# First block: inputs laid out in runs per partition, a new order of loads and modulation units, dummy matmuls

## The reference, cut to what matters

```python
mod = jax.nn.silu(c) @ w_ada[l] + b_ada[l]                      # c: 1 x 1024, w_ada: 1024 x 6144
sh1, sc1, g1, sh2, sc2, g2 = jnp.split(mod, N_MOD, axis=-1)     # six rows of 1024
h = rms_norm(x, norm1_g[l]) * (1.0 + sc1[:, None]) + sh1[:, None]   # x: 512 x 1024
z = h @ w_in[l]                                                 # the first input projection, 1024 x 2048
...
a_out = diff_attention(q, k, v, lam, subln_g[l], lambda_init)   # rotates parts of q and k by cos and sin first
p_out = multiscale_pool(u, w_pool[l], pool_scale[l])
mix = jnp.concatenate([a_out, p_out], axis=-1) @ w_out[l]
```

## Time and profile before

| what | us |
|---|---|
| median of three executions | 1986.4 |
| lowest and highest of them | 1984.96, 1988.44 |
| the profiled execution, its own time | 1988.75 |
| its span, first to last instruction | 1986.9 |
| TensorE busy in it | 1720.8 (87%) |
| VectorE, ACT, GpSimd busy | 856.9, 647.4, 243.6 |

### The profile page before, as it was taken

How to read it: one execution, slowest core, us unless ns; L and a number is a source line. 1 busy time by engine, 2 the same in 40 slices (tenths; PEclk the granted TensorE clock), 3 DMA queues, 4 the chain that set the end, 5 groups by cost and what they waited for, 6 DMA issues and landing times.

```text
span 1986.9 us, 44239 instructions
## 1 busy us (share of the span) xinstructions
PE 1720.8 (87%) x17970; PEld 990.3 (50%) x17970; DVE 856.9 (43%) x1514; ACT 647.4 (33%) x1218; POOL 243.6 (12%) x270
## 2 busy tenths in 40 slices
PE   5998895978777777897889789999988898899996
PEld 2444543544444444444765674354446755753452
DVE  1567524111111111377765763151357747642331
ACT  3414521000000000235544535252245526523442
POOL 0002211111111111005112100001002103000001
PEclk9998996999999999899999999999999999999998
DMA  9758015999999999611000003110211000012101
GB/s 357 264 200 292 1 63 220 383 423 424 424 424 424 424 424 419 236 63 45 4 3 2 3 9 122 43 43 32 80 43 34 4 2 2 4 65 105 43 1 42
DMA packets 75099, 307.76 MB, mean 155 GB/s; under 512 B 10908, under 2 KB 22300, under 8 KB 57888
## 3 DMA queue, kind: packets, MB, share of 16 engines
q1 hardware_dynamic: 63280, 291.98, 37.4%
q0 software_dynamic: 5360, 9.33, 1.3%
q10 hardware_dynamic: 6272, 3.81, 0.7%
HBM read 301.01 MB, written 16.52 MB: 160 GB/s over the span
## 4 chain that ended last, share of the span: by engine, by line
PE 72%; DVE 13%; another core or an unknown queue 6%; ACT 4%; issue 3%; ACTq 1%; DMA 1%; DVEq 0%; POOL 0%; POOLq 0%
PE bank L496 12%; PE bank L2271 12%; PE bank L2287 6%; PE bank L1040 6%; PE bank L549 4%; PE bank L2109 3%; PE bank L2193 3%; PE bank L542 2%; PE bank L1011 2%; PE bank L512 2%; DVE arena L1614 2%; ACT arena L1052 1%; PE bank L2121 1%; PE bank L2133 1%
## 5 line engine op out<-in xcount | busy, mean ns | idle before, releaser
L496 PE MATMUL bank<-hT,arena 128*128 128x512 f32 (+1 forms) x640 | 286.3, 603 | 3.8 <-ACTq L1053 2.4
L2271 PE MATMUL bank<-arena 128*64 128x256 f32 x1792 | 216.8, 399 | 71.2 <-remote 71.2
L2271 PEld LDWEIGHTS bank<-arena 128*64 128x64 f32 x1792 | 134.9, 143 | 163.0 <-issue 113.1
L496 PEld LDWEIGHTS bank<-hT,arena 128*128 128x128 f32 (+1 forms) x640 | 122.4, 193 | 160.4 <-issue 155.9
L2877 DVE COPY arena<-bank 128x256 f32<-128x256 f32 x32 | 13.6, 425 | 329.7 <-PE bank L2279 329.7
L542 PE MATMUL bank<-arena 64*64 64x64 f32 x3200 | 115.1, 223 | 6.8 <-ACT arena L1112 6.0
L2287 PE MATMUL bank<-arena 128*64 128x512 f32 x448 | 102.3, 598 | 16.4 <-remote 16.4
L2531 ACT ACTIVATE arena<-bank 128x512 f32<-128x512 f32 x32 | 19.1, 597 | 293.0 <-PE bank L2287 293.0
L542 PEld LDWEIGHTS bank<-arena 64*64 64x64 f32 x3200 | 105.2, 137 | 13.3 <-issue 6.9
L1052 ACT ACTIVATE arena<-bank 128x512 f32<-128x512 f32 (+2 forms) x124 | 73.2, 590 | 118.5 <-PE bank L496 79.1
L1040 PE MATMUL bank<-arena 128*128 128x512 f32 x256 | 110.4, 593 | 0.0
(11 more groups left out here) (452 smaller groups left out, 2775.4 us busy)
## 6 DMA issues: line engine op xcount, KB each, us to landing
arena<-w_gate SPq DMA_DIRECT2D x28, 2048.0 KB, 30.5
arena<-w_up SPq DMA_DIRECT2D x28, 2048.0 KB, 21.1
arena<-w_down SPq DMA_DIRECT2D x28, 2048.0 KB, 26.3
arena<-w_ada SPq DMA_DIRECT2D x12, 2048.0 KB, 20.0
arena<-w_in SPq DMA_DIRECT2D x10, 2048.0 KB, 9.3
arena<-w_out SPq DMA_DIRECT2D x6, 2048.0 KB, 7.8
arena<-w_in SPq DMA_DIRECT2D x6, 1536.0 KB, 6.5
hT<-w_up SPq DMA_DIRECT2D x4, 2048.0 KB, 20.9
```

Of the source, the lines that this page charges most:

```text
L496: m = pe.matmul(bank[b][0:w, :], slot2(n)[:, k, c:c + w], hT[:, k, :], start=(k == 0), stop=(k == KD - 1))
L2271: mm = pe.matmul(bank[b][c * CAP:(c + 1) * CAP, 0:FE // 2], XT[j][:, k % 4, k // 4, :], e_slot(e_at(e, i), KD)[:, k, c * (FE // 2):(c + 1) ...
```

## The change

- The host lays out w_ada, w_in and w_out of the first block by units, so that a unit is one run of 16 KB in each partition. xT comes as two halves of four tiles, 8 KB in each partition. w_pool and the router's weights (now one tensor) are one run per partition too.
- SP issues the parameters, constants and r1 first, then the two halves of x, each with a semaphore of its own, then the units. ACT issues none of these any more.
- The first four units come in the order 2, 3, 0, 1. TensorE runs for each unit products and then columns, where it ran one unit's products ahead of the columns of the unit before.
- The scale units' columns go to bank 4, and VectorE copies their rows to `mod_rows`. The shift units keep ACT and bank 7. VectorE makes the gains and scales hT when the scale columns are there, and adds the bias of the shift columns afterwards (`shift_moved`).
- ACT squares the even tiles of xT, VectorE the odd ones.
- `keep_busy` adds matmuls of ones with c_sb into bank 7 whose result is not used: two ahead of the sum of squares, and two behind the columns of each scale unit.
- ACT's DMA issues for cos and sin, w_pool and the router's weights (now three) stand behind the eight shift adds.

The core of the diff (left out: renamed semaphores, the signature, and the router's wait, which counts one DMA instead of two):

```diff
--- before.py
+++ after.py
@@ -44,6 +44,8 @@
+SCALE_FIRST = (2, 3, 0, 1)
...
@@ -309,13 +311,13 @@
 
 
         def ada_unit(n):
-            return w_ada[0, :, n * 512:(n + 1) * 512].rearrange("(k p) n -> p k n", p=P)
+            return w_ada[n]
         def in_unit(n):
-            return w_in[0, :, n * 512:(n + 1) * 512].rearrange("(k p) n -> p k n", p=P)
+            return w_in[n]
         def out_unit(n):
-            return w_out[0, :, n * 512:(n + 1) * 512].rearrange("(k p) n -> p k n", p=P)
-        units = [ada_unit(n) for n in range(4)]
-        ada_at, in_at = list(range(4)), []
+            return w_out[n]
+        units = [ada_unit(n) for n in SCALE_FIRST]
+        ada_at, in_at = [SCALE_FIRST.index(n) for n in range(4)], []
         for n in range(4):
             in_at.append(len(units))
             ada_at += [len(units) + 1, len(units) + 2]
@@ -1903,10 +1905,14 @@
 
         @block.sync
         def _(sp):
-            sp.dma_start(xT[:], xT_d.rearrange("(k p) t -> p k t", p=P)).then_inc(sem("x_loaded"), 16)
+            sp.dma_start(p1[:], par1).then_inc(sem("params_loaded"), 16)
+            sp.dma_start(c_sb[:, 0:CN["cosA"][0]], cn[:, 0:CN["cosA"][0]]).then_inc(sem("params_loaded"), 16)
+            sp.dma_start(r1[:], row1.to_broadcast([P, N_R1])).then_inc(sem("params_loaded"), 16)
+            for half in range(2):
+                sp.dma_start(xT[:, 4 * half:4 * half + 4, :], xT_d[half]).then_inc(sem(f"x_loaded{half}"), 16)
             for n, u in enumerate(units):
                 take(sp, slot_free[n % SLOTS])
-                sp.dma_start(slot(n), u).then_inc(slot_full[n % SLOTS], 16)
+                sp.dma_start(ring[:, n % SLOTS, :], u).then_inc(slot_full[n % SLOTS], 16)
             sp.dma_start(y_d, zero_row.to_broadcast([2 * T, D])).then_inc(sem("y_loaded"), 16)
             def weights_unit(e, i, s):
                 w, c = ((w_gate, 1), (w_up, 1), (w_down, 2))[i]
@@ -2074,27 +2080,34 @@
                     q = 32 * (k % 4)
                     mm = pe.matmul(bank[b][q:q + 32, :], small[:, k:k + 1].to_broadcast([P, 32]), slot(ada_at[u])[:, k, :],
                                    start=(k < 4), stop=(k >= 4))
-                mm.then_inc(for_act[b], 1)
+                mm.then_inc((for_dve if u in SCALE_FIRST[:2] else for_act)[b], 1)
             def mod_columns(u):
 
                 take(pe, sem(f"wT_full{u % 2}"))
-                if u % 4 == 0:
-                    take(pe, bank_free[7])
+                b = 4 if u in SCALE_FIRST[:2] else 7
+                if u % 4 == 0 or u == SCALE_FIRST[0]:
+                    take(pe, bank_free[b])
                 for m in range(4):
                     col = 4 * (u % 4) + m
-                    mm = pe.matmul(bank[7][:, col:col + 1], mod_rows[:, u % 2, m * P:(m + 1) * P],
+                    mm = pe.matmul(bank[b][:, col:col + 1], mod_rows[:, u % 2, m * P:(m + 1) * P],
                                    quarters if u < 4 else ones[:, 0:1], start=True, stop=True)
-                if u % 4 == 3:
-                    mm.then_inc(for_dve[7], 1)
+                if u % 4 == 3 or u == SCALE_FIRST[3]:
+                    mm.then_inc(for_dve[b], 1)
                 elif u >= 4:
                     mm.then_inc(sem(f"wT_free{u % 2}"), 1)
 
+            def keep_busy(n):
+
+                pe.wait_ge(bank_free[7], 1)
+                for _ in range(n):
+                    pe.matmul(bank[7][:, :], ones, c_sb[:, 0:512], start=True, stop=True)
+            keep_busy(2)
             sumsq(1, KD, 0)
-            for u in range(4):
+            for u in SCALE_FIRST:
                 mod_products(u)
-                if u > 0:
-                    mod_columns(u - 1)
-            mod_columns(3)
+                mod_columns(u)
+                if u in SCALE_FIRST[:2]:
+                    keep_busy(2)
 
             for n in range(2):
                 s = in_at[n] % SLOTS
@@ -2344,10 +2357,7 @@
         @block.scalar
         def _(act):
             chain = Chain(act, sem("act_chain"))
-            act.dma_start(p1[:], par1).then_inc(sem("params_loaded"), 16)
             late_cols = CN["cosA"][0]
-            act.dma_start(c_sb[:, 0:late_cols], cn[:, 0:late_cols]).then_inc(sem("params_loaded"), 16)
-            act.dma_start(r1[:], row1.to_broadcast([P, N_R1])).then_inc(sem("params_loaded"), 16)
             act.wait_ge(sem("params_loaded"), 48)
             act.activation(small[:, 0:8], par("c", 0, 8), ACT.Silu).then_inc(sem("silu_c"), 1)
 
@@ -2377,19 +2387,21 @@
                 act.sem_inc(slot_free[ada_at[u] % SLOTS], 1)
                 act.sem_inc(sem(f"wT_full{u % 2}"), 1)
 
-            act.wait_ge(sem("x_loaded"), 16)
-            squares(lambda i: xT[:, i, :], KD)
+            for i in range(0, KD, 2):
+                if i % 4 == 0:
+                    act.wait_ge(sem(f"x_loaded{i // 4}"), 16)
+                take(act, sem("sq_free0"))
+                act.activation(sq[:, 0, :], xT[:, i, :], ACT.Square).then_inc(sem("sq_full0"), 1)
             inverse_root(1, 1.0 / D)
-            for u in range(4):
+            for u in SCALE_FIRST[2:]:
                 mod_moved(u)
-            act.dma_start(c_sb[:, late_cols:], cn[:, late_cols:]).then_inc(sem("pool_w_loaded"), 16)
-            act.dma_start(pool_w[:], w_pool[0].rearrange("g c d -> c g d")).then_inc(sem("pool_w_loaded"), 16)
-            act.dma_start(w_router[:, :, 0:4], w_rg[0].rearrange("(k p) n -> p k n", p=P)).then_inc(sem("router_loaded"), 16)
-            act.dma_start(w_router[:, :, 4:36], w_re[0].rearrange("(k p) n -> p k n", p=P)).then_inc(sem("router_loaded"), 16)
-            act.wait_ge(sem("mod_ready"), 1)
+            act.wait_ge(sem("mod_ready"), 2)
             for k in range(KD):
                 act.wait_ge(sem("scaled"), k + 1)
                 act.activation(hT[:, k, :], hT[:, k, :], ACT.Identity, bias=mod[:, k:k + 1]).then_inc(sem("h_ready"), 1)
+            act.dma_start(c_sb[:, late_cols:], cn[:, late_cols:]).then_inc(sem("pool_w_loaded"), 16)
+            act.dma_start(pool_w[:], w_pool).then_inc(sem("pool_w_loaded"), 16)
+            act.dma_start(w_router[:], w_r).then_inc(sem("router_loaded"), 16)
             for i in range(8):
                 b = 2 + i % 2
                 take(act, for_act[b])
@@ -2592,6 +2604,11 @@
             chain(dve.tensor_tensor(small[:, 20:21], small[:, 18:19], small[:, 19:20], ALU.subtract))
             chain(dve.tensor_scalar(small[:, 21:22], small[:, 20:21], 0.2, None, ALU.add))
             chain(dve.tensor_scalar(subln, par("subln_g"), 0.8, None, ALU.mult))
+            for i in range(1, KD, 2):
+                if i % 4 == 1:
+                    dve.wait_ge(sem(f"x_loaded{i // 4}"), 16)
+                take(dve, sem("sq_free1"))
+                dve.tensor_tensor(sq[:, 1, :], xT[:, i, :], xT[:, i, :], ALU.mult).then_inc(sem("sq_full1"), 1)
 
             def modulation(first, b):
                 take(dve, for_dve[b])
@@ -2624,9 +2641,25 @@
                         chain(dve.scalar_tensor_tensor(row, w, small[:, k:k + 1], row, ALU.mult, ALU.add))
                 dve.sem_inc(slot_free[s], 1)
                 dve.sem_inc(sem(f"wT_full{u % 2}"), 1)
-            modulation(0, 7)
+            for u in SCALE_FIRST[:2]:
+                b = 6 * (u % 2)
+                take(dve, for_dve[b])
+                chain(dve.tensor_copy(mod_rows[:, u % 2, :], bank[b][:, :]))
+                dve.sem_inc(bank_free[b], 1)
+                dve.sem_inc(slot_free[ada_at[u] % SLOTS], 1)
+                dve.sem_inc(sem(f"wT_full{u % 2}"), 1)
+            take(dve, for_dve[4])
+            chain(dve.tensor_tensor(mod[:, 8:16], bank[4][:, 8:16], par("b_ada", 8, 8), ALU.add))
+            dve.sem_inc(bank_free[4], 1)
+            dve.sem_inc(sem("mod_ready"), 1)
             gains(0, par("norm1_g", 0, 8))
+            def shift_moved():
+                take(dve, for_dve[7])
+                chain(dve.tensor_tensor(mod[:, 0:8], bank[7][:, 0:8], par("b_ada", 0, 8), ALU.add))
+                dve.sem_inc(bank_free[7], 1)
+                dve.sem_inc(sem("mod_ready"), 1)
             normed(0, 1)
+            shift_moved()
             for i in range(8):
                 dve.wait_ge(sem("raw_ready"), i + 1)
                 if i == 0:
@@ -2659,7 +2692,7 @@
-            dve.wait_ge(sem("router_loaded"), 32)
+            dve.wait_ge(sem("router_loaded"), 16)
```

More of the change, by code:

```diff
@@ L132, in reset, with build @@
         self.n = 0
-def build(nc, xT_d, zero_row, par1, row1, cn, invcnt, w_ada, w_in, w_pool, w_out, w_rg, w_re, w_gate, w_up, w_down,
+def build(nc, xT_d, zero_row, par1, row1, cn, invcnt, w_ada, w_in, w_pool, w_out, w_r, w_gate, w_up, w_down,
           w2, out):
@@ L161, in build @@
             sems[late] = sem(early)
-        first_only = ("silu_c", "raw_ready", "v_ready", "u_ready", "qk_ready", "mix_ready", "x_mixed", "router_loaded",
+        first_only = ("silu_c", "raw_ready", "x_loaded1", "u_ready", "qk_ready", "mix_ready", "x_mixed", "router_loaded",
```

(13 more changed lines are left out.)

## The result

The changed kernel is slower: a median of 1995.89 us in six runs (1993.93 to 1997.45) against 1987.33 of before in six (1984.96 to 1992.68), a ratio of 1.0040 with a 95% interval of 1.0026 to 1.0054. The forecast was 1978.6. The profiled execution took 1995.14 us with a span of 1993.3, 6.4 more than the span before.

A forecast was written before the change was run, and what follows sets the result against it. The start bounds it: waits ahead of the first input projection, including ACT's slow DMA issue, then half clock. An earlier start (4.5 us) and the clock (3.3) gain 7.8, taking the profiled 1988.75 to 1981.0, median 1986.4 to 1978.6; range 1975.8 to 1984.9.

The forecast's parts named there:

- The counts: Pooling on VectorE: up to 3 us of later landing is hidden; cost taken as 0, bound 1 us.
- rival 3: ACT's queue: cos and sin land late behind SP's 16 KB packets, at worst 5 us lost, 1983.9; chance 0.10.
- Transfers: Start's loads at 387 GB/s: parameters land at 4.9, first w_in at 37.4; no unit waited for.
- Sum of squares: TensorE's start: ends at 18.2 instead of 24.25, bounds 17.0 and 22.3.
- Serial units: Four modulation units and two dummy pairs in series on TensorE: 19.9 us, ending at 38.1 against 37.9 before.
- ACT's issues: Ahead of the shift adds: with the 4.94 us issue moved away, first bias add at 38.7, projection at 39.5.
- The clock: First projection tile: TensorE idles 1.4 instead of 6.1 us, tile runs at full clock, gaining 3.3 us.
- Rival 1: First projection tile: clock falls all the same, tile takes 10.1 us again, price 3.2 us, 1981.8; chance 0.25.
- Carrying the lead through: Behind the first tile: later stages, experts' included, move with the compute, so the 7.8 us lead lasts.
- rival 4: Later stages: gain swallowed by a stage released by something that does not move, as experts' transfers; 1986; chance 0.07.
- Rival 2: Start on TensorE: half clock from the sum of squares on, 14.9 us slower, 2001.3; chance 0.08.
- three signs of being wrong: TensorE waits for a unit's landing, clock reads 0.50 behind the columns, or first-move lead is gone at the attention.

The follow-up runs named there:

- e1: The changed kernel with the pooling counts in an area of their own and loaded after the second rotation instead of the eighth: 1988.14 us, ratio 1.0002.
- e2: The changed kernel with w_ada, w_in and w_out read in the old runs of 2 KB: 1987.35 us, ratio 0.9993.
- e3: The kernel before with only the layout by units (runs of 16 KB) for w_ada, w_in and w_out: 2009.45 us, ratio 1.0115.
- e5: The kernel before with only ACT's four DMA issues moved behind its eight shift adds: 1982.65 us, ratio 0.9982.
- e4: e1 with one dummy between products and columns of each unit and one behind the last columns, none behind scale units' columns: 1980.69 us, ratio 0.9968.
- e7: e4 with w_ada, w_in and w_out in the old runs of 2 KB: 1985.95 us, ratio 0.9990.
- e6: e1 without any dummy matmul: 1988.41 us, ratio 0.9995.

## Why the prediction was wrong, step by step

The forecast missed by 17.3 us: 4.8 at the start (7.8 forecast, 3.0 measured; within 0.1, 1.1 from the later sum of squares, 2.0 from the units and 1.8 from the first tile), 8.2 at the pooling, 1.2 behind it, and 3.1 because the profiled execution of before lay 2.35 over its median and that of after 0.75 under its own.

- **The counts, the step that failed.** I took 0 for them with 1 us as the bound, on the ground that a later landing of up to 3 us is hidden. The ground was right: the earlier trace rows has 3.25 us of idling to absorb it. The size was wrong. Measured against the lead of 3.0, the pooling began 9.1 us later (126.85 against 120.79). Of that 3.25 was absorbed there and 0.6 in front of the columns, whose row had been ready that much ahead of TensorE before; 5.2 came out as TensorE's wait, and 8.2 with the clock behind it. I had worked out in rival 3 what runs of 16 KB on SP's queue do to small packets on another, for cos, sin and w_pool, and did not ask it again for the counts, which the earlier trace rows already showed to be late. e1 (an early issue) and e2 (short runs) each take the loss away, and e3 (long runs alone) makes it.
- **Transfers.** The parameters landed at 6.9, not 4.9: r took 5.2 us from its issue, within my bounds of 2.5 and 9.1. I had taken no gain from longer runs; the rate was 430 to 439 GB/s from 10 to 30 us instead of 387. As forecast, no unit was waited for.
- **Sum of squares.** Over at 19.4 instead of 18.2, for the later parameters; the dummies ran at half pace as read (3.75 for two, 3.40 forecast). The granted clock reads 1.00 over them all the same (windows from 8 us on), so in these traces it does not show the slow first stretch; the length of the matmuls does.
- **Serial units.** 19.31 to 41.2, 21.9 instead of 19.9: 0.5 from dummies of 1.96 a pair, 1.6 from the half clock on the last products. The pairs lay on the path as I said, so that the last columns ended later than before's 37.9, as the sum implied.
- **ACT's issues.** Right: nothing stood ahead of the first shift add, and e5 shows what this edit alone is worth: 3.5 us at the first projection matmul, where I had 4.5 for the whole start, 3.8 at the first move, and a ratio of 0.9982. The page that I weighed, the Trainium skill (DMA: Bandwidth & Descriptors, Issuing engines are not separate DMA queues) has issue time as usually small beside the transfer; here the same issue took 4.94, 4.41 and, in e3, 20.57 us, out of 22.2, 20.8 and 24.6 from issue to landing, so for this DMA the measurement decides against it.
- **The clock.** Rival 1 came, and earlier than I had put it: the clock fell on the last unit's products and on the first tile, 1.6 and 1.8 us (8.8 for the tile instead of 7.0). I had counted 3.3 us from the clock as part of the gain; the tile gave 1.3 (8.8 instead of 10.1), and the products took 1.6 away. My argument against it, that it held across the waits between units before, did not carry over: the changed order waits between products and columns of every unit. e4 fills just those waits and reaches 45.1 for the first move, where I had forecast 46.5 for the change.
- **cos, sin and w_pool.** Right as forecast: 57.95 on VectorE lies between 50 and 60 and short of 61.7, and TensorE did not wait.
- **Carrying the lead through.** It held from the first move to the w_out issue, and the lag held from 265 to 812 us, so the experts' stage moves with what stands ahead of it, and rival 4 did not come there. Not to the last microsecond: from the w_up issue to the load of y_scratch before and after took 546.5 us, and e1, e2, e4, e5 and e7, which were ahead, 547.6 to 548.2. But e6, level with before at w_up, took 548.2 as well, so whether it is the lead that is lost there stays open.

Rival 2, half clock throughout, did not come. e6 shows its mechanism, half clock from the second unit on, at a smaller price: with no dummies to pay and the clock back within the first tile, the first move is at 55.05, 0.8 behind before's and far from the 69.0 I had put there. Of the three signs of being wrong that I had named, two came: the clock at 0.50 behind the columns, and the lead gone by the attention.

## What to carry to other kernels

Longer runs for the large transfers can take DMA time from small transfers that are under way beside them on another queue (here the counts, cos and sin, and w_pool took 13.4, 10.5 and 15.7 us to land in the changed kernel, 7.7, 7.2 and 8.2 in e2), and can lengthen the issue of a DMA with many short runs on another engine (here that of w_re, 4.94 us in before and 20.57 in e3): list both before giving a weight stream longer runs, and load small late tables ahead of the stream. A matmul that only keeps the clock up belongs into a wait that is there anyway; behind finished work its whole time is added to the path, and in e1 against e6 it won back no more than that. When a rule has been worked out for one transfer, ask of every other transfer whose landing an engine already waits for whether it applies there too.

## What was not expected of the hardware

How two queues share the DMA engines. The queues' records while the counts and a unit were both under way (queue, kind: packets, MB, share of 16 engines), after, 109 to 119 us; q1 is SP's, q0 GpSimd's:

```profile
q1 hardware_dynamic: 227, 3.24, 78.4%
q0 software_dynamic: 178, 0.60, 20.8%
```

And before, 112.2 to 117 us:

```profile
q1 hardware_dynamic: 529, 1.05, 60.7%
q0 software_dynamic: 154, 0.53, 43.0%
```

The counts got a third of the bytes (0.53 of 1.58 MB) beside runs of 2 KB and a sixth (0.60 of 3.84) beside runs of 16 KB, 110 against 60 GB/s. The Trainium skill (DMA: Bandwidth & Descriptors, Queues, rings and completion order) has each engine go round its queues, a packet of several descriptors at a time. The direction agrees; runs eight times as long changed the ratio of bytes from 2.0 to 5.4, less than eightfold, and by records the queues did not take strict turns either (529 to 154, 227 to 178).

The clock in one program. Up to the first move after and e1 run the same instructions on TensorE, yet the clock fell at 35.4 and 42.2 us in the one and at 24.0, 30.8 and 44.4 in the other, and the first move differs by 1.3 us. What made it fall at one moment and not at another, no run here shows. A single profile therefore prices such a start to within a microsecond or two only; e4, whose clock reads 1.00 from 10 to 60 us, has no such fall in it.
